# Hybrid attention and convolution layer: the first four row tiles of x squared and normalised on two engines, and modulation step 0 put ahead of their normalisation and transpositions

## What is computed

```
c_act = silu(c)
shift, scale, gate = split(c_act @ w_ada + b_ada, 3)
h = rms_norm(x, norm_w) * (1 + scale) + shift
proj = h @ w_in
q, k, v, gate_a, u, gate_b = split(proj, ...)
q = rope(rms_norm(q)) ; k = rope(rms_norm(k))
y_a = sliding_window_attention(q, k, v, sinks) * silu(gate_a)
y_b = silu(layer_norm(causal_conv31(glu(u)))) * silu(gate_b)
out = x + gate * (concat(y_a, y_b) @ w_out)
```

## Time and profile before

| | |
|---|---|
| median of 3 executions | 519.25 us (518.82 to 521.27) |
| the profiled execution, its own time | 518.23 us |
| its span in the profile | 516.1 us |
| TensorE matmuls busy | 432.3 us (84%) |
| TensorE weight loads busy | 337.1 us (65%) |
| VectorE busy | 383.6 us (74%) |
| ScalarE busy | 192.3 us (37%) |
| GpSimd busy | 208.2 us (40%) |
| moved by DMA | 41.93 MB |

### The profile page before, as it was taken

The page is one execution under the profiler, slowest core; times in us unless marked ns, Lnnn a source line. Parts: engine busy times, 40 slices in busy tenths (PEclk is TensorE's granted clock), DMA queues, the critical chain, the costliest instruction groups (busy, mean ns, idle before and its releaser), DMA issues.

```text
span 516.1 us, 5526 instructions
## 1 busy us (share of the span) xinstructions
PE 432.3 (84%) x2025; PEld 337.1 (65%) x2025; DVE 383.6 (74%) x475; ACT 192.3 (37%) x424; POOL 208.2 (40%) x134
## 2 busy tenths in 40 slices
PE   0368899998898198689879689999799996999996
PEld 0256777886677087656656556677477774888885
DVE  0689735499999969999999997939955259982232
ACT  4234439343010015366646757741233334400000
POOL 1441200789616354475456636761403370250000
PEclk9999999998979779699999999999899998899999
DMA  7999610445200000000400303131202040441111
GB/s 239 293 276 309 197 43 0 158 132 167 84 0 6 0 6 7 5 6 1 128 1 1 81 1 83 41 83 41 83 0 81 1 135 28 162 164 62 41 42 61
DMA packets 46374, 41.93 MB, mean 81 GB/s; under 512 B 10425, under 2 KB 41197, under 8 KB 46348
## 3 DMA queue, kind: packets, MB, share of 16 engines
q1 hardware_dynamic: 46348, 41.59, 26.8%
HBM read 37.38 MB, written 4.19 MB: 81 GB/s over the span
## 4 chain that ended last, share of the span: by engine, by line
PE 41%; DVE 41%; issue 7%; ACT 4%; SPq 2%; DMA 2%; POOL 2%; ACTq 0%; DVEq 0%
DVE cacc L1170 15%; DVE z L1170 8%; PE pm L506 6%; PE pm L508 5%; PE pm L507 5%; PE pm L763 3%; PE pm L761 3%; PE pm L762 3%; PE tr L761 2%; PE tr L763 2%; PE tr L762 2%; DMA slab<-in_w_ada 2%; DVE ada_acc L1101 2%; ACT sel L955 2%; DVE nmx L1248 1%
## 5 line engine op out<-in xcount | busy, mean ns | idle before, releaser
L368 POOL TENSOR_TENSOR wts<-raw,wts 128x1024 fp32r<-128x1024 f32 x30 | 84.6, 2836 | 131.8 <-ACT wts L823 131.8
L506 PE MATMUL pm<-h,wts 128*128 128x512 f32 x224 | 94.7, 423 | 12.4 <-POOL wts L368 3.9
L1170 DVE SCALAR_TENSOR_TENSOR cacc<-z,cw,cacc 128x1024 f32<-128x1024 f32 x60 | 98.5, 1687 | 0.2
L508 PE MATMUL pm<-h,wts 128*128 128x512 f32 x224 | 90.3, 403 | 0.0
L507 PE MATMUL pm<-h,wts 128*128 128x512 f32 x224 | 90.2, 403 | 0.0
L1170 DVE SCALAR_TENSOR_TENSOR z<-z,cw 128x1024 f32<-128x1024 f32 x60 | 80.4, 1378 | 0.1
L689 PE MATMUL pm<-wts,h 128*128 128x256 f32 (+1 forms) x128 | 48.6, 380 | 21.8 <-DVE rot L1226 20.4
L506 PEld LDWEIGHTS pm<-h,wts 128*128 128x128 f32 x224 | 43.8, 196 | 28.7 <-issue 7.1
L508 PEld LDWEIGHTS pm<-h,wts 128*128 128x128 f32 x224 | 43.8, 195 | 9.9
L507 PEld LDWEIGHTS pm<-h,wts 128*128 128x128 f32 x224 | 44.1, 197 | 9.2 <-issue 0.8
L823 ACT ACTIVATE wts<-raw 128x1024 fp32r<-128x1024 f32 x30 | 30.7, 1052 | 49.4 <-PE pm L508 26.8
(11 more groups left out here) (179 smaller groups left out, 807.7 us busy)
## 6 DMA issues: line engine op xcount, KB each, us to landing
raw<-in_w_in SPq DMA_DIRECT2D x18, 512.0 KB, 4.1
slab<-in_w_ada SPq DMA_DIRECT2D x16, 512.0 KB, 7.7
xs<-in_x SPq DMA_DIRECT2D x8, 512.0 KB, 6.9
raw<-in_w_ada SPq DMA_DIRECT2D x8, 512.0 KB, 3.7
xr<-in_x SPq DMA_DIRECT2D x8, 512.0 KB, 3.8
out<-xr SPq DMA_DIRECT2D x16, 256.0 KB, 2.0
raw<-in_w_in SPq DMA_DIRECT2D x16, 128.0 KB, 2.7
raw<-in_w_out SPq DMA_DIRECT2D x8, 256.0 KB, 4.0
```

What stands on the lines that cost most here:

```text
L368: gp.tensor_tensor(wts[:, slot, 1, ks, :], raw[:, raw_at["w", i] % 3, :].rearrange("p (k n) -> p k n", k=4), wts[:, slot, 0, ks, :].bitcas ...
L506: pe.matmul(out, hi_w, hi_x, start=first, stop=False)
L508: return pe.matmul(out, hi_w, lo_x, start=False, stop=last)
L1170: ins = dve.scalar_tensor_tensor(out=acc, in0=src, scalar=cw[:, i, j:j + 1], in1=acc, op0=ALU.mult, op1=ALU.add)
```

## The change

- Squares of x, half 0: row tiles 0 and 2 stay with ScalarE (`sum_x`), row tiles 1 and 3 go to VectorE, as one multiply-and-reduce each. The step `mean * 1/D + eps` moves from GpSimd to VectorE (`mean_squares`), for half 1 too; GpSimd keeps the power.
- Normalisation, half 0: row tiles 0, 1 and 2 go to ScalarE, behind the copy of the convolution's weights and ahead of `w_hi(0)`; row tile 3 stays with VectorE.
- VectorE: `ada_sums(0)` comes ahead of the wait for 1/rms, `ada_finish(0)` ahead of `ada_sums(1)`, and `split_h(0)` into the middle of `ada_sums(1)`.
- TensorE: the transpositions of the convolution's weights and `ada_cols(0)` come ahead of `x_transposes(0)`.
- ScalarE: `modulate(0)` comes ahead of `w_hi(2)`.

```diff
@@ -171,7 +171,7 @@
         a_cols, a_ssx, a_h32, a_hi, a_tanh = sem("a_cols"), sem("a_ssx"), sem("a_h32"), sem("a_hi"), sem("a_tanh")
         a_v, a_pt, a_exp, a_qT, a_sel = sem("a_v"), sem("a_pt"), sem("a_exp"), sem("a_qT"), sem("a_sel")
         a_pn, a_att, a_yhi, a_gbc, a_sq, a_ty = sem("a_pn"), sem("a_att"), sem("a_yhi"), sem("a_gbc"), sem("a_sq"), sem("a_ty")
-        a_link = sem("a_link")
+        a_link, a_xn, d_msq = sem("a_link"), sem("a_xn"), sem("d_msq")
 
         d_cact, d_xn, d_ada, d_ab, d_hlo = sem("d_cact"), sem("d_xn"), sem("d_ada"), sem("d_ab"), sem("d_hlo")
         d_glu, d_conv, d_gcol, d_ss, d_rope = sem("d_glu"), sem("d_conv"), sem("d_gcol"), sem("d_ss"), sem("d_rope")
@@ -357,10 +357,9 @@
             gp.tensor_copy(later[:, :], junk[:, 0:P]).then_inc(g_const, 1)
 
             def rms_x(half):
-                gp.wait_ge(a_ssx, 4 * half + 4)
+                gp.wait_ge(d_msq, half + 1)
                 sl = slice(4 * half, 4 * half + 4)
-                link(gp.tensor_scalar(tiny[:, 0:4], ssx[:, sl], 1.0 / D, EPS, ALU.mult, ALU.add))
-                gp.tensor_tensor(rsx[:, sl], tiny[:, 0:4], mhalf[:, 0:4], ALU.pow).then_inc(g_rsx, 1)
+                gp.tensor_tensor(rsx[:, sl], ssx[:, sl], mhalf[:, 0:4], ALU.pow).then_inc(g_rsx, 1)
 
             def w_lo(i):
                 gp.wait_ge(a_hi, i + 1)
@@ -476,7 +475,8 @@
 
                 half, k = idx // KT, idx % KT
                 if k == 0:
-                    pe.wait_ge(d_xn, 4 * half + 4)
+                    pe.wait_ge(a_xn, 3)
+                    pe.wait_ge(d_xn, 4 * half + 1)
                 if idx >= 2:
                     pe.wait_ge(a_h32, idx - 1)
                 for t in range(4):
@@ -513,7 +513,6 @@
                 return three(out, wts[:, slot + 1, 0, k, col:col + P], wts[:, slot + 1, 1, k, col:col + P],
                              h[:, 0, k, sl], h[:, 1, k, sl], k == 0, k == KT - 1)
 
-            x_transposes(0)
             pe.wait_ge(s_cw, 16)
             pe.wait_ge(a_cols, 1)
             for i in range(NCT):
@@ -521,6 +520,7 @@
                                     ident[0:TAPS, 0:TAPS])
             last.then_inc(p_rows, 1)
             ada_cols(0)
+            x_transposes(0)
 
             early = [(pm[:, 0, :], 1, 0), (pm[:, 1, :], 1, P), (pm[:, 2, :], 0, 0), (ps[:, 0, :], 0, P)]
             for k in range(KT):
@@ -810,7 +810,7 @@
             def sum_x(t):
                 act.wait_ge(s_x[t], 16)
                 if t:
-                    act.wait_ge(a_ssx, t)
+                    act.wait_ge(a_ssx, t // 2 if t < 4 else t - 2)
                 act.activation(junk[:, :], xs[:, t, :], ACT.Square, accum_out=ssx[:, t:t + 1]).then_inc(a_ssx, 1)
 
             def w_hi(i):
@@ -839,15 +839,17 @@
 
             act.wait_ge(g_const, 4)
             sum_x(0)
-            sum_x(1)
             sum_x(2)
-            sum_x(3)
             act.wait_ge(p_rows, 2)
             act.activation(cw[:, :, :], pv[:, 64:192].rearrange("p (i t) -> p i t", t=32)[:, :, 0:TAPS], ACT.Copy,
                            scale=0.5).then_inc(a_cols, 1)
-            for i in range(3):
-                w_hi(i)
+            act.wait_ge(g_rsx, 1)
+            for t in range(3):
+                act.activation(xs[:, t, :], xs[:, t, :], ACT.Copy, scale=rsx[:, t:t + 1]).then_inc(a_xn, 1)
+            w_hi(0)
+            w_hi(1)
             modulate(0)
+            w_hi(2)
             w_hi(3)
             for k in range(1, KT):
                 modulate(k)
@@ -1084,14 +1086,14 @@
             def normalize_x(t):
                 dve.tensor_scalar(xs[:, t, :], xs[:, t, :], rsx[:, t:t + 1], None, ALU.mult).then_inc(d_xn, 1)
 
-            def ada_sums(k):
+            def ada_sums(k, first=0, end=8):
 
                 if k == 0:
                     dve.wait_ge(d_cact, 2)
                 dve.wait_ge(s_slab[k % 3], 32 * (k // 3 + 1))
                 if k >= 2:
                     dve.wait_ge(p_ada, k - 1)
-                for ct in range(7):
+                for ct in range(first, min(end, 7)):
                     acc = ada_acc[:, k % 2, ct % 2, :]
                     src = slab[:, k % 3, ct, :, :].rearrange("p a n -> p (a n)")
                     if ct < 2:
@@ -1101,6 +1103,8 @@
                         ins = dve.scalar_tensor_tensor(out=acc, in0=src, scalar=cact[:, ct:ct + 1], in1=acc,
                                                        op0=ALU.mult, op1=ALU.add)
                     ins.then_inc(d_ada, 1)
+                if end < 8:
+                    return
                 dve.wait_ge(d_ada, 8 * k + 7)
                 dve.tensor_tensor(ada_acc[:, k % 2, 0, :], ada_acc[:, k % 2, 0, :], ada_acc[:, k % 2, 1, :],
                                   ALU.add).then_inc(d_ada, 1)
@@ -1120,18 +1124,32 @@
                 dve.tensor_tensor(h[:, 1, k, sl], h32[:, idx % 2, :], h[:, 0, k, sl].bitcast(F32),
                                   ALU.subtract).then_inc(d_hlo, 1)
 
+            def mean_squares(half):
+
+                sl = slice(4 * half, 4 * half + 4)
+                dve.wait_ge(a_ssx, 4 * half + 2)
+                dve.tensor_scalar(ssx[:, sl], ssx[:, sl], 1.0 / D, EPS, ALU.mult, ALU.add).then_inc(d_msq, 1)
+
+            for t in (1, 3):
+                dve.wait_ge(s_x[t], 16)
+                link(dve.tensor_tensor_reduce(h32[:, :, :].rearrange("p a n -> p (a n)"), xs[:, t, :], xs[:, t, :], 1.0, 0.0,
+                                              ALU.mult, ALU.add, ssx[:, t:t + 1]))
+            mean_squares(0)
+            ada_sums(0)
             dve.wait_ge(g_rsx, 1)
-            for t in range(4):
-                normalize_x(t)
-            ada_sums(0)
-            ada_sums(1)
+            normalize_x(3)
             ada_finish(0)
+            ada_sums(1, 0, 4)
+            split_h(0)
+            ada_sums(1, 4)
             for k in range(KT):
-                split_h(k)
+                if k:
+                    split_h(k)
                 if k + 1 < KT:
                     ada_finish(k + 1)
                 if k + 2 < KT:
                     ada_sums(k + 2)
+            mean_squares(1)
             dve.wait_ge(g_rsx, 2)
             for t in range(4, NT):
                 normalize_x(t)
```

## The result

| | before | changed |
|---|---|---|
| median of 11 executions each, on the same chip | 519.52 us | 523.38 us |
| profiled execution, its own time | 518.23 us | 521.41 us |
| its span | 516.1 us | 519.7 us |

The ratio is 1.0067, with a 95% interval of 1.0055 to 1.0078: **slower by 3.5 us** (2.9 to 4.1). One of the changed kernel's 11 executions took 619.63 us at a mean granted clock of 0.67, against 0.94 to 0.95 in the other ten; the ratio goes by those ten, while the medians shown, 3.9 us apart, are of all. The forecast was 524.8 us, 5.3 to 5.5 more than before, with a range from 520.2 to 527.2.

The account below looks back on a forecast made before the run. The first matmul was taken to hang on step 1's sums: 3.75 us undisturbed with the split, plus 1.9, 4.2 and 2.1 for w_lo, ending at 35.1; +5.5 us on 519.25 gave 524.8, range 520.2 to 527.2.

Parts of the forecast that it names:

- four collisions: Step 1's sums on VectorE meet w_lo(0) to w_lo(3), first matmul 5.5 us later: 524.8 us, chance 0.58.
- VectorE keeps the turn: Rival: GpSimd doesn't get in between VectorE's short instructions, w_lo(1) waits until step 1's sums are over: 518.4 us, chance 0.12.
- the rival of three collisions: Fourth raw load lands at 33.0, so w_lo(3) misses step 1's sums and meets step 2's: +3.4, 522.6 us, chance 0.22.
- TensorE's clock: Rival: the 1.3 us lost at the lower clock after 50.30 may go (523.5) or come twice (526.1); only widens the range.
- w_lo(0) starts at 22.9: GpSimd, behind ScalarE's three normalisations: starts at 22.9 instead of 19.48, its rest costing step 1's sums 1.9 us.
- What was costed at nothing: Squares, mean, VectorE's fewer normalisations and the new place of step 0's columns on TensorE: each taken as 0.
- its cover: The over 2.1 us to spare between 1/rms and ScalarE's asking for it, to hold a delay of 2.1 at most.

Follow-up runs that it names:

- the combination: Changed kernel with w_hi(0) and w_hi(1) ahead of ScalarE's normalisations, split_h(0) behind step 1's sums, and w_lo(2) waiting for those sums: 517.02 us, 0.9971.
- w_hi first: Changed kernel with w_hi(0) and w_hi(1) ahead of the three normalisations on ScalarE: 521.96 us, 1.0043.
- split behind the sums: Changed kernel with split_h(0) behind all of step 1's sums instead of in their middle: 522.90 us, 1.0055.
- w_lo(2) waits in the changed kernel: Changed kernel in which GpSimd starts w_lo(2) only when step 1's sums are over, w_lo(3) following it: 519.22 us, 0.9991.
- the combination with w_lo spread: The combination, with w_lo(4) also waiting for step 5's columns and w_lo(5) for split_h(7), 1/rms of half 1 behind it: 516.83 us, 0.9934.
- the kernel before with all w_lo late: Kernel before, with w_lo(2) waiting for step 1's sums, and w_lo(4) and w_lo(5) put behind split_h(7): 518.77 us, 0.9974.

## Why the prediction was right

**The bound.** That the first matmul hangs on step 1's sums and not on step 0's columns held: 11.20 us of idle time on their last addition.

**The chain of consequences** held at each link: normalisations ahead of w_hi(0), w_lo(0) pushed back past the landing of the slab, two queued w_lo taking turns with VectorE one instruction at a time, w_lo(3) getting in as the fourth. The likeliest case (four collisions) came in. The rival in which VectorE keeps the turn fell: at each of three boundaries GpSimd went first. So did the rival of three collisions: the fourth raw load was issued at 24.29 and used at 29.29, 5.0 us later, less than the median of 7.8 that spoke for it. The trace decides this, not the time: 523.4 us lies nearer to that rival's 522.6 than to the 524.8 of four.

**TensorE's clock**, the third rival, neither gave nor took. The stretch at the lower clock moved along with the steps:

```profile
54.20:57.60 3.40, 3.40 (x15) 2.62 (x14) 1.90 (x5) 0.94 (x2) 0.00 (x0) 0.60 1.16 305
```

Step 3 took 5.69 us with it (52.44 to 58.13), against 5.72 before, and there was no second such stretch.

**One sentence of the prediction is too wide.** "While a w_lo runs, the VectorE instruction behind it stands still" holds only for those whose tensors all lie in SBUF. In the trace of the kernel before, one that takes one of its two tensors from PSUM (`ps`) ran inside a w_lo (114.48 to 117.87), in its usual time:

```profile
115.52 0.68 DVE L1149 SCALAR_TENSOR_TENSOR z<-z,ps 128x512 f32<-128x512 f32 x1
```

The eight instructions of that line took 0.63 to 0.69 us each. The sums and the splits have no such operand, so the forecast does not depend on it.

**The sizes.** The forecast was +5.5, the first matmul moved by 4.2, and the time by 3.5:
- "w_lo(0) starts at 22.9" was the term mis-sized. It started at 21.91, so what was left of it behind the landing of the slab cost about 1.15 us (1.50 less 0.35), not 1.9. The copy of the convolution's weights began 0.5 us sooner (17.50 in place of 18.00), and the normalisations took 3.21 us, not 3.45. The copy waits for TensorE's transposition of those weights, and that for their DMA, in the kernel before too:

```profile
17.33 0.50 PEld L520 LDWEIGHTS pv<-ident,cwrows 31*128 31x128 f32 x4 [0.33 <-DMA cwrows<-in_conv_w]
```

  In the changed kernel the same wait ended at 16.83. The new order on TensorE doesn't make it so: in the six other kernels that have this order the wait ended at 17.08 to 17.55. So most of the 1.0 us belongs to the execution that was profiled; in the two others with ScalarE's list as changed, w_lo(0) started at 22.41 and 22.62.
- The slab landed 0.25 us sooner, and the columns took 1.82 us, not 1.99. With the 0.75 us above this is nearly all of the 1.3 us between +5.5 and +4.2.
- The ends of the range are each 0.15 us off the prediction's own terms (519.25 + 3.4 - 2.3 is 520.35, 519.25 + 5.5 + 2.3 is 527.05), which changes nothing.
- The collisions were sized well: 2.43 and twice 2.56 us for one instruction each, 2.1 net.
- Of the 4.2 us 3.8 are left at step 1 (41.76 against 37.95): step 0's matmuls took 0.4 us less, since from the tenth on they followed each other every 0.25 us in place of 0.43, and in the kernel before only from the twelfth. The profile's granted clock is 1.00 in both stretches, so its rows don't say why. From there to step 5 the shift stays 3.8, and the span has 3.6 of it.

**What was costed at nothing** stayed so: the kernel with the normalisations back on VectorE holds all the other moves and is equal to before in the median. The two squares on VectorE took 1.23 us each (1.2 taken); 1/rms was late by no more than its cover. The last row tile of x landed at 12.10 in place of 10.91, which nothing in the change explains; 1/rms still came about 3 us before ScalarE asked for it.

## What to carry to other kernels

Where VectorE and GpSimd both have work, what counts is not how long an operation is but what it lies beside: here each w_lo of 2.35 us cost the VectorE instruction beside it 2.1 us, so it belongs where VectorE waits for something else, or beside instructions of VectorE that take a tensor from PSUM. Before putting work on an engine that looks idle, follow who waits for what it does next; here 3.5 us on ScalarE, 37% busy, cost 3.2 us by moving GpSimd's work out of VectorE's wait for a DMA. And pulling forward one step's result gains nothing where the consumer stands, in its own list, behind the next step's.

## What the runs showed that I had not expected

The loss to TensorE's clock moves about rather than going away. Before, the granted clock was 0.53 from 50.30 to 53.70. In the combination it is full there and low later:

```profile
50.00:54.00 4.00, 4.00 (x26) 3.43 (x24) 3.37 (x10) 2.44 (x4) 0.00 (x0) 1.00 1.15 318
62.00:66.00 4.00, 4.00 (x12) 3.09 (x11) 1.09 (x3) 2.41 (x4) 1.04 (x1) 0.57 0.41 131
```

Both have a gap on TensorE of the same length (1.63 and 1.64 us) ahead of steps 3 and 6, from a split that meets a w_lo, and in each of these two traces one of the gaps was followed by the lower level. Neither one of two nor which one is a rule: in three other traces (w_hi first, split behind the sums, w_lo(2) waits in the changed kernel) both gaps were followed by it.

There is one trace of each kernel, so which gap it is may belong to the execution and not to the kernel. The mean granted clocks on record say that executions of one kernel do differ: those of the combination with w_lo spread run from 518.59 us at 0.939 to 512.69 us at 0.960, those of the kernel before with all w_lo late from 520.09 us at 0.949 to 515.70 us at 0.960. In these two kernels most of the spread between executions goes with TensorE's clock; so a difference of 1 or 2 us between two single executions says little about an edit.
